# One queue's order in an attention phase: four page loads and one head's operands move ahead of value pages

## The chip, the cores and the metric

The kernel runs on one core of one Trainium2 chip. The metric is the device time of one execution in microseconds (us). Before the change it is 3170.54 us, the median of three runs (3167.47 to 3170.95).

## The reference, cut to what matters

One inference step of a hybrid decoder layer, for a prompt of 2064 positions (16 learned tokens and 2048 real ones) and for 8 samples of one new token each, which attend to 4096 cached positions. The part that the change touches is the attention of both:

```python
z = rmsnorm(x) @ w_in                      # q | k | v | forget logit | rnn inputs
# prompt: 8 heads of 64, causal, with a decay from the forget gates
s = q . k * HEAD_DIM**-0.5 + c_q - c_k ;  o = softmax(s) @ v
# samples: k and v of 32 pages of 128 positions for each sample, found by a page table
k_past = cache_k[page_table] ; v_past = cache_v[page_table]
o_sample = softmax(q . [k_past, k] - decay) @ [v_past, v]
x = x + concat(rmsnorm(att), rmsnorm(rnn)) @ w_out
x = x + conv_glu_ffn(rmsnorm(x))
```

## The kernel before

The program has a projection phase (to about 610 us), an attention phase (about 610 to 1390 us) and then the output projection and the feed-forward part. The change is in the attention phase alone.

**Heads and samples.** The attention phase has eight turns, called heads here (numbered from 0). Turn i does prompt head i and, on the same engines, work for the samples. TensorE (PE) walks through 51 score tiles t = 0 to 50 of the prompt head (`pe_head`): scores in transposed form (L2440, L2442), the exponential on ScalarE (L1384), the product with the values (L2456). Between the tiles stand steps from a plan written by hand (`attention_plan`): the row maxima of the next head (L2365, taken by VectorE in L1850) and the work for sample i, which has 32 pages of cached keys and 32 of cached values.

**Cached pages.** A page of keys or of values is a tile of 128 partitions by 512 floats, 256 KB. Pages come in pairs. Key pair g (0 to 15) goes into slot g % 4 of `Kpg`, value pair g into slot g % 4 of `Vpg`. GpSimd (POOL) multiplies a key pair by the query (`pool_products`, L945), and VectorE sums the product (L1863). TensorE takes values in steps `pages(0)` to `pages(7)` (L2480, eight matmuls each), where `pages(n)` uses value pairs 2n and 2n + 1. In a middle head these steps stand after tiles 7, 13, 19, 25, 30, 36, 42 and 48.

**The SP queue.** All of these loads are issued by one in-order instruction stream, that of SyncE (SP), and go through one hardware queue. In the row's names the number of a load runs through a turn: key loads "k" 8 to 15 are key pairs 8 to 15 of sample i + 1, and "k" 16 to 23 are key pairs 0 to 7 of sample i + 2. Value loads "v" 4 to 15 are those pairs of sample i, and "v" 16 to 19 are pairs 0 to 3 of sample i + 1. Three further steps load the values of the next prompt head ("values"), the query of sample i + 2 ("query"), and the queries, keys and decays of prompt head i + 2 ("head", `fetch_head`, L570 to L574: five transfers, four of them of 520 KB). The text below calls them K16, V12 and so on, and two page transfers of 256 KB make one such pair. The waits and issues of a pair are:

```python
def fetch_keys(s, g):
    e.wait_ge(kpp, 16 * s + g - 3)        # POOL's product of the pair that held the slot
    fetch_pages("cache_k", Kpg, kg_ld, s, g)
def fetch_cached_values(s, g):
    e.wait_ge(vd, 16 * s + g + 1)         # PE's step that read the slot's last pair
    fetch_pages("cache_v", Vpg, vg_ld, s, g)
# in sync_head, for "head":
    e.wait_ge(prep, 7 * i + 14)           # POOL has copied the operands of head i + 1
    e.wait_ge(dec, i + 3)
    fetch_head(i + 2)
```

So K16 waits for the product of key pair 12 of sample i + 1 ("product 12" below), K19 for product 15, V12 and V13 for `pages(4)`, V14 and V15 for `pages(5)`. When the number of a pair is a multiple of four, `page_ids` first loads eight page numbers from SBUF into registers of the queue, after the wait and before the transfer. TensorE waits in `pages(n)` for both of its value pairs (`vg_ld`).

**The order.** `load_order` gives each load a due time, in units of tiles, and sorts. The order of a middle head around the change is: K14 (21.5), K15 (23), V10 and V11 (25.5), K16 (25.6), K17 (27.1), K18 (28.6), K19 (30.1), V12 and V13 (30.5), V14 and V15 (36.5), head (36.6), K20 (37) and so on. The first head has its own order. Of the last two turns, turn 6 leaves out K16 and later and "head", and turn 7 has neither, so that the lines of the change act in turns 1 to 5.

Of the kernel before, what the change touches and what calls it, by code (L numbers as in the profile page):

```python
# [199 lines left out]
def load_order(first, last):  # L200

    found = []
    for b in range(PAGES // 4):
        at = 27 + 23 * (2 * b + 1) // 15 if first else 5 + (37 if last else 43) * (2 * b + 1) // 15
        found += [(at + 0.5, "v", 2 * b + 4), (at + 0.5, "v", 2 * b + 5)]
    for n in range(4 if first else 8, 24):
        if first:
            at = 26 + 1.5 * (n - 4)
        else:
            at = 5.2 + 1.5 * (n - 8) if n < 14 else 21.5 + 1.5 * (n - 14) if n < 16 else 25.6 + 1.5 * (n - 16) if n < 20 else 37 + 1.5 * (n - 20)  # L210
        found.append((at, "k", n))
    found += [(20, "values", 0), (23, "head", 0), (31, "query", 0)] if first else \
        [(14, "values", 0), (17, "query", 0), (36.6, "head", 0)]
    return [step[1:] for step in sorted(found)]


# [4 lines left out]
def build(nc, a, out):  # L221
    ctx = ExitStack()
    with ctx:
# [313 lines left out]
        def _(e):  # L537
# [147 lines left out]
            for g in range(4):  # L685
                fetch_keys(1, g)
            sync_head(0, 0, load_order(True, False), 2)
            for ii in range(2):
                for v in range(2):
                    sync_head(2 * ii + 1 + v, 1 - v, load_order(False, False), 2)  # L690
            sync_head(5, 1, load_order(False, False), 2)
            sync_head(6, 0, load_order(False, False), 1)
            sync_head(7, 1, load_order(False, True), 0)
# [2048 lines left out]
```

## Time and profile before

| what | value |
|---|---|
| time, median of three runs | 3170.54 us |
| the profiled execution: its time | 3170.95 us |
| its span in the profile | 3169.2 us |
| its mean granted TensorE clock | 0.963 |
| busy: PE, VectorE (DVE), ScalarE (ACT), POOL | 94%, 45%, 24%, 39% |
| turns 2 to 5 of the attention phase | 907.81 to 1242.48 us |

Times in a row are from the start of the span. A row of a timeline gives start and length in us, then engine, line, operation, output and input; in brackets the idle time before it and what ended it. A turn is taken here from the start of POOL's first instruction for the next head (`memset` of `QA`, L917, which waits for TensorE's last tile) to the next such start.

### The profile page before, as it was taken

Reading aid. Unit: us, or ns where it says so; the run is one execution under the profiler, and the core shown is the slowest. Engines: PE = TensorE matmul, PEld = TensorE weight load, DVE = VectorE, ACT = ScalarE, POOL = GpSimd, SP = SyncE. Lnnn points to the kernel's source line nnn. Section 1 sums busy time; section 2 is a strip of 40 time slices with the busy share of each in tenths; the row PEclk is TensorE's granted clock in tenths of the full one; section 3 lists DMA queues with packets and bytes.
Section 4 is the critical chain, followed back from the end, with each engine's and each line's share of the span. In section 5 each row is a group of like instructions: output and inputs, shape, how many; then the busy total and the mean of one; then the engine's idle time right before and its main releaser. Section 6 shows DMA issues by size and latency. Waiting matters only on the chain.

```text
span 3169.2 us, 44502 instructions
## 1 busy us (share of the span) xinstructions
PE 2964.1 (94%) x15701; PEld 2595.8 (82%) x15701; DVE 1415.2 (45%) x1912; ACT 756.9 (24%) x1533; POOL 1232.5 (39%) x588
## 2 busy tenths in 40 slices
PE   4999999777799999979999999999999999999998
PEld 4899999743455555549999999999999998999998
DVE  5312444476677776424154454445444552212221
ACT  7000233322233333332020000000000003443442
POOL 1111110267767676326762222222222214444443
PEclk9999999878799999989999999999999999999999
DMA  7212333447778888563451111111111115555553
GB/s 227 75 69 88 108 114 106 124 144 227 235 235 260 253 248 242 181 205 99 137 158 42 54 47 45 42 53 48 47 43 49 52 49 183 194 186 174 190 195 106
DMA packets 249030, 422.45 MB, mean 133 GB/s; under 512 B 44693, under 2 KB 152418, under 8 KB 244370
## 3 DMA queue, kind: packets, MB, share of 16 engines
q1 hardware_dynamic: 167986, 322.58, 32.3%
q10 hardware_dynamic: 80616, 97.07, 9.1%
q8 instruction: 74, 1.21, 0.2%
q0 software_dynamic: 288, 1.05, 0.1%
q14 instruction: 66, 0.54, 0.0%
HBM read 337.21 MB, written 83.46 MB: 133 GB/s over the span
## 4 chain that ended last, share of the span: by engine, by line
PE 82%; DVE 6%; POOL 5%; ACT 3%; issue 2%; DMA 2%; SPq 1%; ACTq 0%; POOLq 0%; DVEq 0%
PE PS L2572 35%; PE PS L2237 14%; PE PS L2456 5%; PE PS L2660 5%; PE PS L2662 5%; PE PS L2661 5%; POOL prod L945 2%; PE PS L2440 2%; PE PS L2365 2%; PE PS L2480 1%; PE PS L2442 1%; PE PS L2563 1%; DVE MP L1850 1%; DVE YT L2186 1%; DVE scw L1863 1%
## 5 line engine op out<-in xcount | busy, mean ns | idle before, releaser
L2572 PE MATMUL PS<-MH,VS 128*128 128x416 f32 (+1 forms) x4000 | 1080.4, 351 | 2.8 <-issue 2.7
L2572 PEld LDWEIGHTS PS<-MH,VS 128*128 128x128 f32 x4000 | 749.3, 188 | 12.8 <-issue 4.2
L2572 PE MATMUL PS<-ML,VS 128*128 128x416 f32 (+1 forms) x2000 | 699.7, 350 | 0.0
L2572 PEld LDWEIGHTS PS<-ML,VS 128*128 128x128 f32 x2000 | 376.0, 188 | 2.6 <-issue 0.8
L1097 POOL TENSOR_TENSOR DL<-DR,DH 128x1408 fp32r<-128x1408 f32 x80 | 258.6, 3232 | 287.6 <-ACT DH L1521 287.5
L945 POOL TENSOR_TENSOR prod<-Kpg,qb 128x1024 f32<-128x1024 f32 x128 | 302.5, 2363 | 124.8 <-DVE scw L1900 42.2
L1026 POOL CAST VS<-VR 128x1024 fp32r<-128x1024 f32 x52 | 62.8, 1209 | 689.1 <-PE PS L2572 687.5
L2456 PE MATMUL PS<-PT,VA 128*65 128x416 f32 (+16 forms) x816 | 326.6, 484 | 4.4 <-ACT PT L1384 3.2
L2660 PE MATMUL PS<-GH,DH 128*128 128x416 f32 (+1 forms) x880 | 315.5, 359 | 15.0 <-DVE GL L2168 7.6
L2662 PE MATMUL PS<-GH,DL 128*128 128x416 f32 (+1 forms) x880 | 311.3, 354 | 0.0
L2661 PE MATMUL PS<-GL,DH 128*128 128x416 f32 (+1 forms) x880 | 309.9, 352 | 0.0
L1384 ACT ACTIVATE PT<-PS 128x416 f32<-128x416 f32 (+16 forms) x408 | 186.3, 459 | 438.2 <-PE PS L2442 277.3
L2237 PE MATMUL PS<-XH,WH 128*128 128x416 f32 (+1 forms) x800 | 290.5, 363 | 0.0
L2237 PE MATMUL PS<-XL,WH 128*128 128x416 f32 (+1 forms) x800 | 280.9, 351 | 0.0
L2237 PE MATMUL PS<-XH,WL 128*128 128x416 f32 (+1 forms) x800 | 280.4, 351 | 0.0
L2365 PE MATMUL PS<-KA,QA 68*128 68x512 f32 (+3 forms) x360 | 213.8, 618 | 61.9 <-DVE MP L1850 42.6
L1494 ACT ACTIVATE GC<-GC 128x416 f32<-128x416 f32 x110 | 60.8, 553 | 839.0 <-DVE GC L2121 760.9
L1850 DVE TENSOR_REDUCE MP<-PS 128x1 f32<-128x512 f32 (+3 forms) x360 | 205.3, 599 | 100.6 <-PE PS L2365 60.6
L2151 DVE TENSOR_TENSOR GP<-PS,R 128x416 f32<-128x416 f32 x110 | 64.8, 592 | 400.0 <-PE PS L2572 399.6
L877 POOL CAST WH<-WR 128x1024 fp32r<-128x1024 f32 x21 | 22.6, 1076 | 427.3 <-PE PS L2237 392.4
L2660 PEld LDWEIGHTS PS<-GH,DH 128*128 128x128 f32 x880 | 167.1, 190 | 19.7 <-issue 13.3
L2365 PEld LDWEIGHTS PS<-KA,QA 68*128 68x128 f32 (+1 forms) x360 | 71.5, 199 | 134.8 <-DVE MP L1850 73.7
(289 smaller groups left out, 4434.6 us busy)
## 6 DMA issues: line engine op xcount, KB each, us to landing
Kpg<-in_cache_k SPq DMA_DIRECT2D x256, 256.0 KB, 4.8
Vpg<-in_cache_v SPq DMA_DIRECT2D x256, 256.0 KB, 4.4
DR<-in_w_down SPq DMA_DIRECT2D x80, 704.0 KB, 4.1
gT<-GO ACTq DMA_DIRECT2D x110, 208.0 KB, 2.0
VR<-in_w_up SPq DMA_DIRECT2D x44, 512.0 KB, 3.4
GRb<-gT SPq DMA_DIRECT2D x31, 416.0 KB, 4.8
WR<-in_w_stream SPq DMA_DIRECT2D x21, 512.0 KB, 3.5
GRa<-gT SPq DMA_DIRECT2D x24, 416.0 KB, 5.5
```

Of the source, the lines that this page charges most:

```text
L945: e.tensor_tensor(prod[:, g % 4], Kpg[:, g % 4], qb[:, v].unsqueeze(1).to_broadcast([P, 2, DATT]), ALU.mult).then_inc(kpp, 1)
L1097: e.tensor_tensor(DL[h][:], DR[:, h], DH[h][:].bitcast(F32), ALU.subtract).then_inc(d_lo, 1)
L1384: e.activation(PT[0:kr, t % 3, 0:n], PS[0:kr, (u + t) % 2, 0:n], ACT.Exp, scale=0.125).then_inc(ex, 1)
L1850: e.tensor_reduce(MP[0:rows, qt, pc:pc + 1], PS[0:rows, banks[p % len(banks)], 0:n], AX.X, ALU.max).then_inc(mx, 1)
L2151: e.tensor_tensor(GP[u][:, 2 + j * BW:2 + (j + 1) * BW], PS[:, j, 0:BW], R2[:, cols(j)], ALU.mult)\
L2237: mm = e.matmul(PS[:, j, 0:full(j)], w[:, u, k], x[:, k, j * BW:j * BW + full(j)], start=(k == 0 and q == 0), stop=(k == KC - 1 and q == 2))
L2365: mm = e.matmul(o[:, 0:n], QA[0:HD + 4, v, qt * P:qt * P + rows], KA[0:HD + 4, v, k0:k0 + n], start=True, stop=not diag)
L2456: e.matmul(PS[0:HD + 1, 4 + (u + j) % 2, o:o + n], VA[0:kr, u, kt], PT[0:kr, t % 3, 0:n], start=(kt == 0), stop=t in ENDS).then_inc(pv, 1)
L2572: mm = e.matmul(PS[:, j, 0:full(j)], w[:, u, k], x[:, k, j * BW:j * BW + full(j)], start=(k == 0 and q == 0), stop=(k == KC - 1 and q == 2))
L2660: e.matmul(PS[:, v, 0:full(j)], DH[h][:, k], GH[:, r, m, 0:full(j)], start=(kk == 0), stop=False)
L2661: e.matmul(PS[:, v, 0:full(j)], DH[h][:, k], GL[:, r, m, 0:full(j)], start=False, stop=False)
L2662: e.matmul(PS[:, v, 0:full(j)], DL[h][:, k], GH[:, r, m, 0:full(j)], start=False, stop=(kk == FC - 1))\
```

## The change

Two due times of every head but the first change. K16 to K19 are due 1.1 tiles earlier, and "head" is due at 30.2 in place of 36.6. Nothing is computed, loaded or waited for that was not before.

```diff
@@ load_order
-            at = 5.2 + 1.5 * (n - 8) if n < 14 else 21.5 + 1.5 * (n - 14) if n < 16 else 25.6 + 1.5 * (n - 16) if n < 20 else 37 + 1.5 * (n - 20)
+            at = 5.2 + 1.5 * (n - 8) if n < 14 else 21.5 + 1.5 * (n - 14) if n < 20 else 37 + 1.5 * (n - 20)
         found.append((at, "k", n))
     found += [(20, "values", 0), (23, "head", 0), (31, "query", 0)] if first else \
-        [(14, "values", 0), (17, "query", 0), (36.6, "head", 0)]
+        [(14, "values", 0), (17, "query", 0), (30.2, "head", 0)]
```

The order becomes K14, K15, **K16**, V10, V11, K17, K18, K19, **head**, V12, V13, V14, V15, K20.

## Rows read from the trace of the kernel before

**Rows 1.** The page's chain that ended last, by engine.

```profile
PE 82%; DVE 6%; POOL 5%; ACT 3%; issue 2%; DMA 2%; SPq 1%; ACTq 0%; POOLq 0%; DVEq 0%
```

**Rows 2.** Windows of turns 2 to 4: length, busy times, PEclk, DMA share, GB/s.

```profile
907.81:990.15 82.34, 76.45 (x383) 42.69 (x383) 59.90 (x83) 28.20 (x63) 59.44 (x23) 0.98 0.81 245
990.15:1074.92 84.77, 79.25 (x383) 44.40 (x383) 60.13 (x83) 28.19 (x63) 59.42 (x23) 0.94 0.84 258
1074.92:1157.64 82.72, 77.22 (x383) 43.52 (x383) 60.16 (x83) 28.19 (x63) 59.43 (x23) 0.96 0.81 246
```

**Rows 3.** Timeline of the SP queue in turn 3 (V10, K16, V12, head, K20).

```profile
1035.20 1.99 SPq L605 DMA_DIRECT2D Vpg<-in_cache_v  x4
1040.05 5.92 SPq L605 DMA_DIRECT2D Kpg<-in_cache_k  x8
1048.84 4.25 SPq L605 DMA_DIRECT2D Vpg<-in_cache_v  x8
1053.28 0.47 SPq L570 DMA_DIRECT2D Qst<-qT  x1
...
1055.52 1.23 SPq L574 DMA_DIRECT2D Kst<-kT  x1
1059.97 4.19 SPq L605 DMA_DIRECT2D Kpg<-in_cache_k  x8
```

**Rows 4.** DMA issues: all; last, windows 1044:1046 and 1062:1066. KB, us to landing.

```profile
Vpg<-in_cache_v SPq DMA_DIRECT2D x256, 256.0 KB, 4.4
Qst<-qT SPq DMA_DIRECT2D x16, 520.0 KB
...
Kpg<-in_cache_k SPq DMA_DIRECT2D x2, 256.0 KB, 3.5
...
Kpg<-in_cache_k SPq DMA_DIRECT2D x4, 256.0 KB, 10.2
```

**Rows 5.** Timeline of POOL: product 15 of turn 1, product 12 of turns 2 to 5.

```profile
872.18 2.37 POOL L945 TENSOR_TENSOR prod<-Kpg,qb 128x1024 f32<-128x1024 f32 x1 [1.64 <-DVE scw L1863]
...
951.87 2.37 POOL L945 TENSOR_TENSOR prod<-Kpg,qb 128x1024 f32<-128x1024 f32 x1 [0.29 <-POOL prod L945]
...
1034.17 2.37 POOL L945 TENSOR_TENSOR prod<-Kpg,qb 128x1024 f32<-128x1024 f32 x1 [0.29 <-POOL prod L945]
...
1119.25 2.37 POOL L945 TENSOR_TENSOR prod<-Kpg,qb 128x1024 f32<-128x1024 f32 x1 [0.59 <-POOL prod L945]
...
1201.67 2.37 POOL L945 TENSOR_TENSOR prod<-Kpg,qb 128x1024 f32<-128x1024 f32 x1 [0.29 <-POOL prod L945]
```

**Rows 6.** Timeline of PE: `pages(6)` of turns 1 to 5, `pages(5)` and an idle of turn 2.

```profile
895.29 1.06 PE L2480 MATMUL PS<-Vpg,scw 128*32 128x512 f32 x8
...
964.75 1.07 PE L2480 MATMUL PS<-Vpg,scw 128*32 128x512 f32 x8
973.33 0.42 PE L2365 MATMUL PS<-KA,QA 68*32 68x512 f32 x1 [2.46 <-DVE MP L1850]
977.61 1.07 PE L2480 MATMUL PS<-Vpg,scw 128*32 128x512 f32 x8
...
1062.36 1.10 PE L2480 MATMUL PS<-Vpg,scw 128*32 128x512 f32 x8
...
1145.10 1.07 PE L2480 MATMUL PS<-Vpg,scw 128*32 128x512 f32 x8
...
1229.95 1.07 PE L2480 MATMUL PS<-Vpg,scw 128*32 128x512 f32 x8
```

**Rows 7.** DMA view, one value per us, from 950, 1035, 1117 and 1200 us.

```profile
GB/s 356 268 328 246 387 410 346 393 287 258 275 223 326 373 352 250 4 182 371 92 209 356 383 404 375 216 225 216 208 241 200 224 237 145 216 305 385 391 385 385
...
GB/s 283 367 303 354 348 410 367 350 262 297 358 295 340 84 43 242 346 168 315 377 369 388 239 179 241 233 200 233 225 208 218 175 219 254 379 389 387 383 383 385
...
GB/s 295 279 361 401 307 313 303 387 197 272 307 217 268 361 291 303 49 35 248 252 262 359 289 348 403 243 241 216 241 241 216 208 258 184 157 152 359 387 389 385
...
GB/s 389 191 320 348 336 340 340 389 348 277 350 260 264 381 352 242 12 170 315 246 111 377 279 238 341 285 202 241 250 258 266 225 277 194 132 158 301 385 383 389
```

## The prediction

> **What bounds the kernel now.** I read the page first: the chain that ended last lies on TensorE for 82% of the span, on DMA for 2% [rows 1]. Then the windows of turns 2 to 4 [rows 2]: in 82.34, 84.77 and 82.72 us TensorE is busy for 76.45 to 79.25 us, VectorE and POOL for about 60. Turns 2 and 3 have the same 383 matmuls and differ by 2.43 us; the granted clock is 0.98 in one and 0.94 in the other, so that time comes from stretches at 1.2 in place of 2.4 GHz. Turn 5 repeats turn 3 (84.84 us). The loads keep the DMA engines busy for 81 to 84% of a turn: they are hidden, but not by much. So the question is which transfer lands last before TensorE needs it. For that I read the SP queue of turn 3 [rows 3], the sizes and landings [rows 4], POOL's products, which release the key loads [rows 5], TensorE's page steps, which consume the value pairs [rows 6], and the traffic microsecond by microsecond [rows 7].
>
> **The change part by part.** It removes and adds nothing. It moves seven instructions' worth of issue on SP: K16 (two transfers) past V10 and V11, and the five transfers of "head" past V12 to V15.
>
> *The waits of what is moved.* K16 waits for product 12, which ends in turn 3 at 1034.17 + 2.37 = 1036.54 us [rows 5]. "head" waits for POOL's copies and for a decay row, which stand ahead of product 12 and at the start of the turn: no wait at its new place. The page numbers cost time on SP: V11 is out at 1035.20 + 1.99 = 1037.19, K16 follows at 1040.05; K19 is out at 1045.97, V12 follows at 1048.84; both times 2.9 us [rows 3].
>
> *New issue times in turn 3.* K16 at 1036.5 + 2.9 = 1039.4 in place of 1040.05. V10 and V11 wait behind it: out by about 1042.5 in place of 1037.2, over 5 us later. K19 waits for product 15, three products of 2.37 + 0.29 us behind product 12, and so stays where it is. "head" starts at 1046.1 in place of 1053.28. Its issue takes 1053.28 to 1056.75, 3.5 us [rows 3], so V12 is issued at 1052.4 in place of 1048.84. V15 is then out at 1056.7, and K20 leaves at 1059.9, as now: SP's own work is only permuted.
>
> *What SP's order means for landings.* The key transfers issued in 1044:1046 land after 3.5 us, those issued in 1062:1066, behind "head", after 10.2 us [rows 4]. And the traffic of turn 3 shows "head" as a block: twelve values from 1057 on, between 175 and 254 GB/s, mean 219 (the tail of V15 lies in the first of them), and then the key pages at 379 to 389 [rows 7]. Transfers are served in the order of issue. "head" is 4 x 520 KB and a small one, 2.15 MB [rows 4]; at 219 GB/s that is 9.8 us. Two value pairs are 4 x 256 KB = 1.05 MB, at 385 GB/s 2.7 us.
>
> The Trainium skill ("DMA: Bandwidth & Descriptors", section "Queues, rings and completion order") says that each DMA engine consumes the descriptors of a ring in order. By that rule V12 can't overtake "head", and the landings of 3.5 and 10.2 us agree.
>
> *When the queue is drained of K19.* Now the traffic falls to 4 to 84 GB/s in the slices from 966, 1048, 1133 and 1216 us of turns 2 to 5 [rows 7]; that is the pause in which "head" will be put. After the change V10 and V11 are served between K16 and K17. Traffic resumes about 1.3 us after an issue (V12 at 1048.84, 242 GB/s in the slice from 1050). From K16's first byte on there are 12 transfers, 3.15 MB. The thirteen slices before the pause average 333 GB/s in turn 3 and 302 in turn 4; pages alone reach 385. So 9.45 us, with 8.2 and 10.5 as bounds. K16's issue is product 12's end plus 2.9: 957.1, 1039.4, 1124.5 and 1206.9 [rows 5]. Plus 1.3 and 9.45 us the queue is drained at 967.9, 1050.2, 1135.3 and 1217.7.
>
> *When V13 lands, and when it is needed.* "head" 9.8 us, V12 and V13 2.7, and 0.5 for completion (the last pair of K19 is issued at 1045.1 to 1045.6, lands 3.5 later, just behind the end of traffic): 13.0 us. V13 lands at 980.9, 1063.2, 1148.3 and 1230.7. `pages(6)` starts now at 977.61, 1062.36, 1145.10 and 1229.95 [rows 6]. TensorE waits there for 3.3, 0.8, 3.2 and 0.8 us, with the bounds of the drain -1.25 and +1.05 for each: 2.0 to 4.3, 0 to 1.8, 1.9 to 4.2, 0 to 1.8. The sum is 8.1 us, between 3.9 and 12.1. In turn 1 K19 is late anyway (product 15 ends at 872.18 + 2.37 = 874.55), out at about 876.0; traffic of "head" from 878 on, V13 at 891 against 895.29: no wait.
>
> Behind the waiting matmul stand the last eight tiles of the turn, and POOL, whose next turn waits for the last of them. TensorE has no idle of its own in that stretch to swallow the wait, so it counts in full. V14 and V15 land 2.7 us behind V13 and are needed ten us later.
>
> *V10 and V11.* Six transfers (1.57 MB) from K16's first byte: in turn 2 958.4 + 4.7 + 0.5 = 963.6 us against 964.75 for `pages(5)` [rows 6]. 1.1 us of slack, 0.6 at 300 GB/s. Turn 2 has the least slack of the four. I cost it at nothing; if the cover is gone it is some tenths of a us in one turn.
>
> *The clock.* In turn 2 TensorE has already idled 2.46 us ahead of 973.33 [rows 6]; the new wait comes 4 us behind that. One more stretch at the lower level costs what turns 2 and 3 differ by, 2.4 us. The trace does not show whether it comes. From below it is nothing, from above 4.8 us for turns 2 and 4; I take one of the two, +2.4.
>
> *What it gives.* "head" lands 8 us earlier, but it is needed only in the next turn, K20 to K23 likewise; TensorE and POOL wait for none of them in turns 2 to 5. The pause in the traffic is filled and nobody gets it: nothing.
>
> Sum: 8.1 + 2.4 = 10.5 us on the profiled execution's 3170.95 us, which is 0.4 us above the median. Against the median: 3170.5 + 10.5 = 3181.0 us, +0.33%. A measurement of this kernel can tell about 0.2%, 6.3 us, from no change.
>
> **The rivals.**
>
> *Hidden anyway (3171 us, chance 0.28).* If "head" goes faster behind a short queue than behind a long one, V13 is in time. It needs 3.3 us less in turns 2 and 4, so 6.5 in place of 9.8 us, 330 GB/s in place of 219. All four turns show the low plateau, whatever else ran, which speaks against it; for it speaks that SP's issue of V12 is late by only 3.6 us, and that bounds on the drain take 1.25 of the 3.3. With half of it left, the sum falls below 6.3 us too.
>
> The Trainium skill (same page, "Specifications") gives 358 GB/s for HBM per core. At that rate "head" would take 6.0 us and V13 would land before all four `pages(6)`: 3171. The trace's 219 GB/s decides against it.
>
> *The value pairs of `pages(5)` too (3189 us, chance 0.08).* V10 and V11 are the pairs delayed most. If pairs are served at 300 GB/s or less and K16's product is a us later, as VectorE's sums can make it, `pages(5)` of turn 2 waits as well, K19 drains at the late bound and the sum is 12.1 + 4.8 + about 1.5 = 18 us.
>
> *Faster (3161 us, chance 0.07).* The stretches at the lower clock depend on where TensorE's idles fall. The share lost is 6%, 4% and 6% of turns 3, 4 and 5, 5.1 + 3.3 + 5.1 = 13.5 us; at 2.43 us of time for the 3.4 that turns 2 and 3 differ by, all of it is worth 9.6 us. A shift of 2 to 3 us could do away with it: 3161. It decides once two of the three turns run at full clock. Against it: idles of 2.3 to 2.7 us ahead of `pages(6)` and in the middle of the turn are left as they are, and a wait is added.
>
> **How the numbers follow.** The forecast has 0.57 (with its own range of 3174 to 3188: 3.9 to 12.1 us of waits and 0 to 4.8 us of clock), hidden 0.28, `pages(5)` too 0.08, faster 0.07. Of the forecast's 0.57 about 0.05 stays below 6.3 us. So slower by over 0.2%: 0.52 + 0.08 = 0.60. Faster by over 0.2%: 0.07 and 0.02 from shifts of the clock in the hidden case, 0.09. Within: 0.31. The range goes from 3168 (the hidden case with a stretch of clock to the good) to 3190.
>
> **What the profile after would show.** On SP in turn 3: K16 ahead of V10, "head" from 1046 on directly behind K19, V12 some 3.6 us later relative to product 12. In the traffic: no pause, the 220 GB/s block from the drain on, 8 us earlier. On TensorE: an idle ahead of L2480 at `pages(6)`, ended by the DMA of Vpg, of about 3 us in turns 2 and 4, under 2 in 3 and 5, none in 1. The turns: 2 and 4 at 86 to 88 us, 3 and 5 at 85 to 87. POOL and VectorE unchanged within a turn. The prediction is wrong if `pages(6)` shows no idle (the plateau was not the price of "head"), if `pages(5)` does, or if turns change length at equal waits, which would be the clock.

## The result and the profile after

The changed kernel takes 3194.76 us, the median of five runs (3184.25 to 3201.24), against 3170.95 us for the kernel before (3167.47 to 3174.86, five runs). The ratio is 1.0077, with a 95% interval of 1.0059 to 1.0094: slower by 0.8%, 24 us. The forecast was 3181.0 us with a range up to 3190. The direction and the place were right, the size was too small by more than half.

The windows of turns 2 to 5 of the changed kernel, as [rows 2] for before (length, busy PE, PEld, DVE, ACT and POOL with their counts, PEclk, DMA share, GB/s):

```profile
910.40:1000.37 89.97, 79.90 (x383) 44.31 (x383) 60.29 (x83) 28.24 (x63) 59.48 (x24) 0.91 0.78 235
1000.37:1089.61 89.24, 78.44 (x383) 43.34 (x383) 60.24 (x83) 28.24 (x63) 59.46 (x23) 0.92 0.77 237
1089.61:1178.17 88.56, 79.06 (x383) 43.54 (x383) 60.28 (x83) 28.24 (x63) 59.50 (x24) 0.92 0.77 239
1178.17:1266.81 88.64, 79.11 (x383) 43.52 (x383) 60.24 (x83) 28.24 (x63) 59.45 (x23) 0.92 0.77 238
```

All four turns are long now. Before, the stretch from the start of turn 2 to the end of turn 5 was 1242.48 - 907.81 = 334.7 us; now it is 1266.81 - 910.40 = 356.4 us: 21.7 of the 24 us lie here. These are two single executions. In the profiled executions of the seven variants below that measured like the kernel before, the same stretch took 335.5 to 341.4 us, and in a second one of the changed kernel 354.0, so this share is at the upper end of what a pair of executions can show. VectorE and POOL do the same work in the same busy time, and the granted clock is 0.91 to 0.92.

The timeline of TensorE, `pages(6)` of turns 2 to 5, as [rows 6]:

```profile
985.86 1.93 PE L2480 MATMUL PS<-Vpg,scw 128*32 128x512 f32 x8 [4.52 <-DMA Vpg<-in_cache_v]
...
1075.58 1.93 PE L2480 MATMUL PS<-Vpg,scw 128*32 128x512 f32 x8 [5.28 <-DMA Vpg<-in_cache_v]
...
1163.92 1.94 PE L2480 MATMUL PS<-Vpg,scw 128*32 128x512 f32 x8 [3.96 <-DMA Vpg<-in_cache_v]
...
1252.48 1.94 PE L2480 MATMUL PS<-Vpg,scw 128*32 128x512 f32 x8 [4.02 <-DMA Vpg<-in_cache_v]
```

The bracket is what was not there before: TensorE stands still for the value pages, 17.8 us in all. The second column shows the other half: the eight matmuls take 1.93 us, where they took 1.06 to 1.10 in [rows 6]. They run at 1.2 GHz.

The SP queue of turn 3, as [rows 3] (turn starts at 1000.37):

```profile
1044.24 6.25 SPq L605 DMA_DIRECT2D Kpg<-in_cache_k  x6
1050.75 1.95 SPq L605 DMA_DIRECT2D Vpg<-in_cache_v  x4
1052.95 3.47 SPq L605 DMA_DIRECT2D Kpg<-in_cache_k  x6
1056.62 0.47 SPq L570 DMA_DIRECT2D Qst<-qT  x1
...
1062.61 4.20 SPq L605 DMA_DIRECT2D Vpg<-in_cache_v  x8
1069.66 4.69 SPq L605 DMA_DIRECT2D Kpg<-in_cache_k  x8
```

K14 to K16, V10 and V11, K17 to K19, "head", V12 to V15, K20 to K23. "head" starts 56.25 us into the turn (forecast 1046.1 - 990.15 = 55.95), V12 at 62.24 (forecast 62.25).

The traffic of the changed kernel, one value per us from 1042 us (turn 3) and from 1130 us (turn 4), as [rows 7]:

```profile
GB/s 6 199 334 160 320 383 395 283 61 289 301 150 311 383 344 352 385 387 411 214 216 241 208 241 224 200 225 178 222 203 354 387 385 385 389 389 385 385 385 326
...
GB/s 25 254 322 295 283 342 367 227 0 0 209 348 275 248 352 336 358 399 369 452 158 233 233 208 216 258 208 250 181 204 231 389 389 389 383 379 393 389 389 381
```

The pause that stood between K19 and V12 is gone. The block of "head" (about 215 GB/s) runs from 1061 to 1072 and from 1150 to 1161 us, eleven values each, and directly behind it come the value pages at 385. The last two or three of the eleven values already carry page packets, as slow as the block: 150 to 160 ns for 2 KB, against about 90 ns right behind it. By the trace V13 lands at 1163.78 us in turn 4, and TensorE starts at 1163.92. The page's chain now has DMA in it, as [rows 1]:

```profile
PE 77%; POOL 5%; DVE 5%; DMA 4%; SPq 3%; ACT 3%; issue 3%; ACTq 0%; POOLq 0%; DVEq 0%
```

What the wait does to the clock is seen in the stretch from the start of `pages(6)` to the end of the turn. First the changed kernel, turns 2 to 5:

```profile
985.86:1000.37 14.51, 14.51 (x73) 7.31 (x74) 2.80 (x8) 5.83 (x14) 0.00 (x1) 0.85 0.69 241
1075.58:1089.61 14.03, 14.03 (x73) 7.07 (x74) 2.80 (x8) 5.83 (x14) 0.00 (x0) 0.88 0.70 249
1163.92:1178.17 14.25, 14.25 (x73) 7.23 (x74) 2.80 (x8) 5.82 (x14) 0.00 (x1) 0.87 0.71 260
1252.48:1266.81 14.33, 14.33 (x73) 7.22 (x74) 2.79 (x8) 5.83 (x14) 0.00 (x0) 0.87 0.71 260
```

and one of the four of the kernel before, which took 12.53 to 12.56 us each:

```profile
977.61:990.15 12.54, 12.54 (x74) 6.63 (x74) 3.35 (x10) 5.81 (x14) 0.32 (x1) 1.00 1.02 276
```

The same work, TensorE busy throughout in both, 12.5 us at full clock and 14.0 to 14.5 behind a wait. The four together are 57.12 against 50.17 us: 7.0 us.

### The profile page after: what moved, and what is told of

It is laid out like the page before. It is cut to its first block, busy times and chain, and to the rows that moved or that the text cites. A ratio compares the mean times of both kernels' runs of the same rounds, so it can differ in the third digit from the quotient of the medians.

```text
span 3196.1 us, 44502 instructions
## 1 busy us (share of the span) xinstructions
PE 2971.9 (93%) x15701; PEld 2598.0 (81%) x15701; DVE 1414.3 (44%) x1912; ACT 757.4 (24%) x1533; POOL 1233.0 (39%) x588
## 4 chain that ended last, share of the span: by engine, by line
PE 77%; POOL 5%; DVE 5%; DMA 4%; SPq 3%; ACT 3%; issue 3%; ACTq 0%; POOLq 0%; DVEq 0%
PE PS L2572 35%; PE PS L2237 14%; PE PS L2660 4%; PE PS L2662 4%; PE PS L2661 4%; PE PS L2456 4%; POOL prod L945 2%; DMA Vpg<-in_cache_v 2%; SPq L605 1%; PE PS L2480 1%; PE PS L2563 1%; PE PS L2440 1%; PE PS L2365 1%; PE PS L2442 1%; SPq L598 1%
## 5 line engine op out<-in xcount | busy, mean ns | idle before, releaser
L2365 PEld LDWEIGHTS PS<-KA,QA 68*128 68x128 f32 (+1 forms) x360 | 71.0, 198 | 132.6 <-DVE MP L1850 71.6
```

What stands on the lines that cost most here:

```text
L2365: mm = e.matmul(o[:, 0:n], QA[0:HD + 4, v, qt * P:qt * P + rows], KA[0:HD + 4, v, k0:k0 + n], start=True, stop=not diag)
```

## The experiments

Times are medians beside the kernel before on the same chip. There that kernel's own runs spread wider than in the result: 3163 to 3188 us in 29 runs (median 3175.87) beside the keys alone, "head" alone, "head" between V13 and V14 and the half-size block, 3168 to 3184 in 23 runs (3174.13) beside the two other places of "head" and the two repeats, 3167 to 3184 in 23 runs (3173.26) beside the two kernels with wide transfers. Ratios with their intervals are read, not single times.

**The two moves apart.** First the keys alone:

```diff
-  else 21.5 + 1.5 * (n - 14) if n < 16 else 25.6 + 1.5 * (n - 16) if n < 20 else ...
+  else 21.5 + 1.5 * (n - 14) if n < 20 else ...
```

> K16 ahead of V10 and V11, "head" left behind V15. Theory Q (the queue serves in order of issue, and TensorE waits for V12 and V13 behind "head"): no wait before pages(6), V10 and V11 land in time for pages(5), 3171 us, within 4 us of the kernel before. Rival K (the key move costs a part by itself, through V10 and V11 or a later drain of the queue): waits before pages(5) or pages(6), 3175 to 3183 us.

3172.55 us, ratio 0.9983 (0.9970 to 0.9996). The longest wait for value pages in turns 1 to 5 is 0.16 us. The move by itself costs nothing, and V10 and V11, 5 us later, are in time.

Then "head" alone:

```diff
-        [(14, "values", 0), (17, "query", 0), (36.6, "head", 0)]
+        [(14, "values", 0), (17, "query", 0), (30.2, "head", 0)]
```

> Only "head" moves, ahead of V12. Theory Q: the last pair of K19 lands 58.7 to 59.3 us into the turn as in the kernel before, V13 13.0 us later, at 71.7 to 72.3, against a pages(6) that would start at 69.9: a wait of 1.9 to 2.4 us in each of turns 2 to 5, each with 1.5 us of slower clock behind it, less 3.3 us that turns 3 and 5 arrive earlier: about +11, 3182 us. If "head" alone is the whole loss: 3195 us. If the loss needs both moves: 3171 us.

3193.44 us, ratio 1.0050 (1.0037 to 1.0062), by the ratio 16 us. TensorE's timeline at `pages(6)`, turns 1 to 5:

```profile
890.12 1.94 PE L2480 MATMUL PS<-Vpg,scw 128*32 128x512 f32 x8 [2.58 <-DMA Vpg<-in_cache_v]
...
977.87 1.94 PE L2480 MATMUL PS<-Vpg,scw 128*32 128x512 f32 x8 [3.84 <-DMA Vpg<-in_cache_v]
...
1066.80 1.07 PE L2480 MATMUL PS<-Vpg,scw 128*32 128x512 f32 x8 [1.49 <-DMA Vpg<-in_cache_v]
...
1152.51 1.93 PE L2480 MATMUL PS<-Vpg,scw 128*32 128x512 f32 x8 [3.11 <-DMA Vpg<-in_cache_v]
...
1243.42 1.93 PE L2480 MATMUL PS<-Vpg,scw 128*32 128x512 f32 x8 [4.49 <-DMA Vpg<-in_cache_v]
```

"head" makes the waits. In turns 2 to 5 they sum to 12.9 us, against 17.8 with both moves: V10 and V11 are served before K16, and in turns 2 to 4 the first packets of "head" start 57.3 to 58.1 us into the turn, against 59.6 to 59.7. The key move, free by itself, makes the other dearer. In the turn with the short wait the eight matmuls take 1.07 us, in the others 1.93: behind 1.5 us of wait the clock stayed up, behind 2.6 us and more it fell. What I expected was 11 us; turn 1, where I had none, waits too.

**Where in the queue "head" may stand.** Between V13 and V14:

```diff
-        [(14, "values", 0), (17, "query", 0), (36.6, "head", 0)]
+        [(14, "values", 0), (17, "query", 0), (33, "head", 0)]
```

> The kernel before with "head" between V13 and V14. Theory Q: V13 lands at 64.6 us of the turn as before, V15 12.5 to 13 us later at 77.4, and pages(7) starts at 80.2: no wait, 3171 us within 4. Rival S (what costs is SP's issue of the value pairs later by 3.6 us, or the busier queue as such): 3178 us or more, since V14 and V15 are issued later by as much.

3175.63 us, ratio 0.9997 (0.9982 to 1.0013). No wait for value pages in turns 1 to 5. V14 and V15 stand behind the block as V12 and V13 do in the change, but they are needed ten us later.

K16 early as in the change, and "head" behind V12, V13 and K19:

```diff
-  else 21.5 + 1.5 * (n - 14) if n < 20 else 37 + 1.5 * (n - 20)
+  else 21.5 + 1.5 * (n - 14) if n < 19 else 30.6 if n < 20 else 37 + 1.5 * (n - 20)
...
-        [(14, "values", 0), (17, "query", 0), (30.2, "head", 0)]
+        [(14, "values", 0), (17, "query", 0), (30.8, "head", 0)]
```

> K16 early as in the change, then K18, V12, V13, K19, "head", V14, V15: "head" is issued as early as 58 us into the turn, in the pause of the traffic, but V12 and V13 are ahead of it. Theory Q: V13 lands by 60 us, V15 by 74 against pages(7) at 80: no waits, the time of the kernel before within 4 us, and no gain from the early landing, since nothing waits for "head". Rival S (an early "head" costs as such): 3180 us or more.

3176.53 us, ratio 1.0008 (0.9995 to 1.0021), no wait for value pages in turns 1 to 5. But "head" is not as early as I expected: it is issued 61.0 to 61.4 us into the turn, against 56.3 in the changed kernel and 62.7 to 64.4 before. V15 lands at 79.0 to 81.2 us, where I expected 74, at the least 1 us ahead of `pages(7)`. So this run shows that V12 and V13 are safe ahead of "head". What an early "head" costs or brings by itself it does not show; the wide transfers below do.

Ahead of V10:

```diff
-        [(14, "values", 0), (17, "query", 0), (36.6, "head", 0)]
+        [(14, "values", 0), (17, "query", 0), (25.2, "head", 0)]
```

> The kernel before with "head" between K15 and V10. Theory Q: the cost follows "head" to the pairs behind it. K15 lands 49 us into the turn, the block takes 10 to 11 us, V11 lands at about 62, against pages(5) at 57 to 58: a wait of about 5 us there in turns 1 to 5, none before pages(6), with the slower clock behind it +25 to +33 us, 3196 to 3204 on 3171. Rival: if the loss is particular to pages(6), because TensorE idles for VectorE shortly ahead of it, this order costs less than 10 us.

3190.10 us, ratio 1.0048 (1.0029 to 1.0067), 16 us. The waits moved to `pages(5)`, here of turns 3 and 4 in TensorE's timeline:

```profile
1059.41 1.93 PE L2480 MATMUL PS<-Vpg,scw 128*32 128x512 f32 x8 [6.77 <-DMA Vpg<-in_cache_v]
...
1146.71 1.93 PE L2480 MATMUL PS<-Vpg,scw 128*32 128x512 f32 x8 [5.32 <-DMA Vpg<-in_cache_v]
```

With 3.17, 6.46 and 5.18 in turns 1, 2 and 5 they sum to 26.9 us, as expected, and yet the time rises by 16. The view of TensorE's waits has the answer (waits in total, times, longest), of this kernel:

```profile
PE PS L2480 <- DMA Vpg<-in_cache_v: 34.8, 9, 6.8
PE PS L2365 <- DVE MP L1850: 31.9, 30, 4.7
```

and of the kernel before:

```profile
PE PS L2365 <- DVE MP L1850: 42.6, 35, 4.7
```

The wait before `pages(5)` stands ahead of an idle in which TensorE waits for VectorE's maxima (2.46 us in [rows 6], 2.3 in the other turns). While TensorE waits for pages, VectorE catches up, and that idle is gone in all five turns: 10.7 us less. Behind `pages(6)` there is no such idle, so there a wait counts in full. My expectation of this run missed it.

**The block's length.** Half the rows, everything else in place (half of the queries and keys of prompt heads 2 to 7 is left out):

```diff
-                e.dma_start(Qst[0:HD], qT[bass.ds(h * HD, HD), :]).then_inc(st_ld, 16)
+                e.dma_start(Qst[0:rows], qT[bass.ds(h * HD, rows), :]).then_inc(st_ld, 16)
...            # rows = 32, the same for the other three
```

> The changed kernel with half the rows in each of the four large transfers of "head" (32 of 64; the other half of the queries and keys of prompt heads 2 to 7 is left out), all issues where they are. Theory Q: the block in the queue shrinks by 4.9 us, V13 lands at 70.4 in place of 75.3 us of the turn, the waits before pages(6) go from 4.0 to 5.3 us down to 0 to 0.5 us: 3171 to 3176 us. Rival S (SP issues V12 and V13 too late): issue times are unchanged, the waits stay at 4 us or more, 3195 us.

3172.94 us, ratio 0.9988 (0.9977 to 0.9999). The traffic from 930 us, whose block starts at 964 us:

```profile
GB/s 162 281 334 240 363 275 180 308 449 300 270 150 188 285 53 68 258 268 303 260 287 385 277 0 92 389 215 209 274 361 381 393 393 446 255 212 191 231 204 204
```

The block has the same height and is over at 972 us: eight values in place of eleven, of which the last three are mostly page packets. V13 lands 71.5, 68.7, 70.6 and 69.9 us into turns 2 to 5, against 75.3, 75.1, 74.2 and 74.2, and the waits before `pages(6)` are 0.17 us or nothing. In turns 2 to 4 TensorE also came late, at 71.6 to 73.7 us; turn 5 is the clean case, where it came at 69.9. SP issues V12 5.0 us behind the first transfer of "head", 6.0 us in the changed kernel: the shorter transfers are issued a little faster, but that is 1 us, and V13 lands 3.6 to 6.4 us earlier. The last rows of "head" are served at 65.0 us or later here, when V12 would have been issued at either pace. SP's later issue is not what costs.

The same bytes in another shape (128 neighbouring rows to 128 partitions; the prompt attention of heads 2 to 7 is not the reference's):

```diff
-                e.dma_start(Qst[0:HD], qT[bass.ds(h * HD, HD), :]).then_inc(st_ld, 16)
-                e.dma_start(Qst[HD:P], qT[bass.ds(h * HD, HD), :]).then_inc(st_ld, 16)
+                e.dma_start(Qst[:], qT[bass.ds((h - 1) * HD, P), :]).then_inc(st_ld, 32)
...            # Kst2 likewise
```

> The changed kernel with the four 64-row transfers of "head" as two of 128 rows to 128 partitions, the same bytes, in the same place (the source is 128 neighbouring rows, so that one half of the operands belongs to the head before: the prompt attention of heads 2 to 7 is not the reference's). If the 220 GB/s of the block come from its 64-partition shape: the block runs near 385 GB/s, 5.6 us in place of 9.8, V13 lands 4 us earlier, the waits before pages(6) fall to 0 to 1.5 us, 3172 to 3180 us. If they come from rows of 8320 bytes or from the source tensor: block and waits as in the changed kernel, 3195 us.

3176.04 us, ratio 1.0012 (1.0001 to 1.0023), in place of 1.0073 to 1.0077. The traffic of turn 3, from 1045 us, with "head" issued from 1053.7 on:

```profile
GB/s 332 361 111 254 322 350 307 367 358 369 352 381 429 433 433 391 433 350 393 395 375 387 297 315 324 279 301 309 266 264 74 49 268 361 281 94 2 0 0 164
```

No block at 215 any more, and no wait before `pages(6)` in turns 2 to 5. V13 lands at 69.2 to 70.8 us. SP also issues V12 1.5 to 2.0 us earlier, behind three transfers in place of five, but the rows of "head" are served until 65.1 us or later, so V12 would have been issued in time at either pace. So the rate comes neither from the source tensor nor from the length of the rows, which are both unchanged. But the destination was not all that changed: each source row is read once here, twice in the changed kernel. The trace of the kernel before has a control for that, both lines from its view of windows. The first is the store of a prompt head's output (`mixT`, L1371: 64 partitions, rows of 8256 bytes, each row moved once), the second a load of 128 rows of 8320 bytes to 128 partitions (`RC`, L1281):

```profile
1347.00:1349.00 2.00, 1.88 (x10) 1.13 (x9) 0.00 (x0) 1.43 (x3) 0.00 (x0) 1.00 0.98 198
431.00:433.00 2.00, 2.00 (x14) 1.93 (x13) 0.32 (x1) 2.00 (x3) 0.00 (x0) 1.00 1.00 420
```

With the DMA engines equally busy (0.98 and 1.00) it is 198 against 420 GB/s, so a repeated source is not needed for the low rate. A row's packet takes about 600 ns in "head" of 64 rows and 642 in that store, and about 320 in the wide transfers and in that load.

> The kernel before with the same two 128-row transfers (the same part of the reference left out). Whatever the block's rate, nobody waits for anything behind it in the order before: within 5 us of the kernel before, ratio 0.998 to 1.002.

3175.03 us, ratio 1.0000 (0.9986 to 1.0015): in the order before, a shorter block is worth nothing. The pair of wide kernels also shows what an early "head" is worth. Its last packet ends 65.1 to 67.6 us into the turn in the first and 73.2 to 75.5 in this one, and the first is no faster (1.0012 against 1.0000).

**Repeats.** The changed kernel and the keys alone once more.

> The changed kernel once more, beside the next three. 18 to 30 us above the kernel before; waits of 4 to 5.5 us before pages(6) in turns 2 to 5.

3196.26 us, ratio 1.0073 (1.0056 to 1.0090), with waits before `pages(6)` of 0.69, 5.77, 4.31 and 4.47 us in turns 2 to 5; turn 2 came to `pages(6)` late here, behind a stretch at the lower clock. The expectation of 4 us or more in each turn held in three of four.

> K16 ahead of V10 and V11 alone, again. If its ratio of 0.998 was the chance of the clock's stretches: 0.996 to 1.004 here, with the sign open. If it is a gain of the key move: 0.997 to 0.999 again.

3173.45 us, ratio 0.9999 (0.9984 to 1.0014). The 0.9983 of the first time did not come back; the key move alone makes no difference. No version ran that clearly beats the kernel before.

## Why the prediction was right or wrong

**Right: the mechanism.** Transfers are served in the order of issue, "head" fills the pause, V12 and V13 stand behind it, TensorE waits at `pages(6)`, and the wait counts in full. The head-only kernel, the half-size block and the wide block show each link. The issue times came out within 0.3 us. `pages(5)` shows no wait, as costed. The early landing of "head" gives nothing, as the two wide kernels show. Of the rivals, "hidden anyway" needed the block at 330 GB/s; the wide shape ran it there, and the time was nearly that rival's. The Trainium skill's 358 GB/s per core ("DMA: Bandwidth & Descriptors", "Specifications") is exceeded by the page transfers (379 to 389 in [rows 7]) and by the wide ones (433), and is far from the 215 of the narrow ones; what decides here is the shape, which the prediction did not ask about.

**Wrong: the size of the wait, 17.8 us in place of 8.1.** Two terms.

*"`pages(6)` starts now at 977.61, 1062.36, 1145.10 and 1229.95".* I kept these times for the new kernel. Two of them, of turns 3 and 5, are 2 us later than the others, in turn 3 behind a stretch with a granted clock of 0.72 (1020.9 to 1033.1 us). That is no property of those turns: with the keys alone, turns 3 and 5 reach `pages(6)` at 69.8 us and turns 2 and 4 at 73.7 and 72.3. In the changed kernel TensorE reaches `pages(6)` at 70.9, 69.9, 70.3 and 70.3 us of the turn (start less wait), where I had used 69.8, 72.2, 70.2 and 72.3. That makes the waits longer by 3.0 us in all, but the turns shorter by as much: in the total it cancels.

*"13.0 us" from the drain to V13, and the drain.* V13 lets TensorE start 75.5, 75.2, 74.3 and 74.3 us into the turn; I had 73.1, 73.1, 73.4 and 73.1. That is 6.6 us over the four turns. The traffic shows most of it in the block, eleven us long where I had 9.8. I divided its bytes by its rate, although twelve values of the plateau stood in [rows 7], and took the rest for the tail of V15, in the first value. By the packets of the trace the rest is at the other end: the last four of the twelve values carry pages issued behind "head", at the low rate, beside its last rows. From its first to its last packet "head" took 11.0 to 12.7 us in turns 2 to 5 before, and 11.2 to 12.3 in the changed kernel. The drain was right in turn 4 (60.4 us into the turn in both) and 0.6 us late in turn 3.

**Wrong: "I take one of the two, +2.4" for the clock.** All four waits were followed by slower clock, with 7.0 us in all. The two terms, 6.6 and 4.6 us above the forecast, make 21.7 in place of 10.5: 17.8 of waits and 7.0 of clock, less 3.0 for arriving earlier. I had treated the price of the clock as a coin toss beside the wait. Here it came with the wait: in turns 1 to 5 of all the kernels each wait for value pages above 2.5 us had it, and those of 0.7 to 1.5 us did not. The wait is not the only thing that brings it. TensorE also stands for 2.3 us for VectorE shortly ahead of `pages(6)`, and in turns 2 and 4 of the kernel with V12 and V13 ahead of "head" the clock was low at `pages(6)` without a wait for pages:

```profile
976.51 1.94 PE L2480 MATMUL PS<-Vpg,scw 128*32 128x512 f32 x8
```

How the two idles share in it no run separates.

**Not settled.** The profiled execution is 26.9 us longer than the one before, 5.2 more than turns 2 to 5. Of that 2.9 lie ahead of turn 1, where the two kernels are the same, and 2.6 behind turn 5. The medians differ by 23.8. The profiled execution of the kernel before was the fastest of all twelve behind turn 5, with 1926.7 us; the variants that measured like it took 1928.7 to 1935.7 there. So I count the 5.2 us as such spread; no run was made to test it.

## What to carry to other kernels

A transfer that nobody waits for still has a price: its service time, paid by whatever is issued behind it on the same queue and is needed soon. Here V12 and V13 paid, and V14 and V15, needed ten us later, did not. Before moving a load earlier, take the block's length from the traffic itself, not from bytes over a rate, and compare the landing of the next loads with the earliest time that their consumer can have, not with the time that one trace shows. And a long wait of TensorE is priced with the slower clock behind it: 1.5 to 2.0 us here for each of 4.0 to 5.3 us. An idle of its own that follows can swallow part of the wait, 2.3 us a turn with "head" ahead of V10.

## What the runs showed of the hardware

Four transfers of 64 rows of 8320 bytes to 64 partitions moved about 215 GB/s with the DMA engines fully busy; the same bytes as two transfers to 128 partitions ran at 350 to 433. With 32 rows to 32 partitions the height was about the same as with 64. I had not expected the number of partitions to matter by nearly two, and it was the whole difference between 1.0075 and 1.0012.
